# Transposing activations, softmax rows and GLA keys with DMAs on SP's queue instead of TensorE matmuls, in a hybrid decoder layer

## The reference, cut to what matters

```
xn = rmsnorm(x)
q,k,v,gz,og,u,ga,gb = split(xn @ w_in)            # GLA with chunked scan, pooling branch
o  = rmsnorm(GLA(q,k,v,log_sigmoid(gz @ w_gk_up + b)/16)) * silu(og)
h  = x + (sig(ga)*(o @ w_a) + sig(gb)*(pool_mix(u) @ w_b)) @ w_out
h  = h + softmax(rmsnorm(h) @ w_xq @ K_mem^T / 16) @ V_mem @ w_xo
h  = h + relu(rmsnorm(h) @ w_up)**2 @ w_down
y  = rmsnorm(h)
```

## Time and profile before

| what | value |
|---|---|
| median of the runs shown | 1297.88 us |
| lowest of them | 1295.64 us |
| profiled execution | 1297.93 us |
| its span on the slowest core, which the trace shows | 1296.4 us |
| spans of the 8 cores | 1286.1 to 1296.4 us |
| TensorE (PE) busy | 1261.8 us, 97% |
| DVE busy, ACT busy | 655.0 us, 651.5 us |

### The profile page before, as it was taken

One profiled execution on the slowest core, in us unless ns is written; L12 is line 12 of the kernel. 1 busy time (PEld: TensorE's weight loads), 2 busy tenths in 40 slices (PEclk: granted clock), 3 DMA queues, 4 the chain that ended last, 5 costly groups with the idle time before them and its releaser, 6 DMA issues.

```text
span 1296.4 us, 23207 instructions; the slowest of 8 cores (1286.1 to 1296.4 us)
## 1 busy us (share of the span) xinstructions
PE 1261.8 (97%) x8490; PEld 646.2 (50%) x8490; DVE 655.0 (51%) x1088; ACT 651.5 (50%) x1333; POOL 68.4 (5%) x131
## 2 busy tenths in 40 slices
PE   6899999999999999999999999999999999999997
PEld 4444556444455554444544455644455544454453
DVE  3564755241458765444575346723244754444346
ACT  3555966556587743032246278855557753120304
POOL 1110000000000000000000010100100000000000
PEclk7999999999999999999999999999999999999999
DMA  8979369353929569786779596758871333342503
GB/s 173 185 161 181 68 126 184 55 99 71 223 82 227 136 163 163 125 145 137 142 166 203 94 150 120 138 110 138 143 191 35 64 66 66 65 74 58 98 2 138
DMA packets 33675, 160.93 MB, mean 124 GB/s; under 512 B 4598, under 2 KB 5246, under 8 KB 22156
## 3 DMA queue, kind: packets, MB, share of 16 engines
q0 software_dynamic: 18112, 104.29, 48.9%
q1 hardware_dynamic: 15452, 55.15, 12.5%
HBM read 241.63 MB, written 22.80 MB: 204 GB/s over the span
## 4 chain that ended last, share of the span: by engine, by line
PE 93%; DMA 3%; DVE 1%; issue 1%; ACT 1%; DVEq 0%; ACTq 0%; SPq 0%
PE pb L818 83%; PE pb L829 6%; PE pb L849 3%; PE pb L839 1%; DMA land_113<-xp 1%; DMA xst_93<-xp 1%; DMA xst_89<-xp 1%; DMA xst_91<-xp 0%; ACT xn_102 L868 0%; DVE S L889 0%; DVE xh L889 0%; DVE xn_102 L889 0%; DVE xn_101 L889 0%; ACT stat L868 0%; DVE xn_102 L884 0%
## 5 line engine op out<-in xcount | busy, mean ns | idle before, releaser
L889 DVE SCALAR_TENSOR_TENSOR xh<-pb,r_178,xh 128x512 f32<-128x512 f32 x128 | 95.6, 750 | 91.6 <-PE pb L818 91.3
L818 PE MATMUL pb<-actT,wt_45 128*128 128x512 bf16 x448 | 101.4, 379 | 0.0
L818 PE MATMUL pb<-actT,wt_44 128*128 128x512 bf16 x448 | 100.4, 379 | 0.0
L868 ACT ACTIVATE tmp_98<-pb 128x512 f32<-128x512 f32 (+1 forms) x48 | 28.3, 590 | 111.0 <-PE pb L818 108.6
L818 PE MATMUL pb<-actT,wtG 128*128 128x512 bf16 x320 | 72.8, 379 | 0.0
L818 PE MATMUL pb<-actT,wt_43 128*128 128x512 bf16 x320 | 72.5, 379 | 0.0
L818 PEld LDWEIGHTS pb<-actT,wt_45 128*128 128x128 bf16 x448 | 43.1, 98 | 50.5 <-issue 0.4
L818 PEld LDWEIGHTS pb<-actT,wt_44 128*128 128x128 bf16 x448 | 43.1, 98 | 49.7
L878 DVE TENSOR_TENSOR xh<-pb,xh 128x512 f32<-128x512 f32 x64 | 44.2, 691 | 46.8 <-PE pb L818 46.6
L868 ACT ACTIVATE tmp_95<-pb 128x512 f32<-128x512 f32 (+1 forms) x49 | 28.5, 581 | 75.1 <-PE pb L818 60.9
L818 PE MATMUL pb<-wt_45,actT 128*128 128x512 bf16 x256 | 59.3, 379 | 0.6 <-DVE xn_101 L889 0.4
(11 more groups left out here) (559 smaller groups left out, 2378.2 us busy)
## 6 DMA issues: line engine op xcount, KB each, us to landing
wt_44<-wu POOLq DMA_DIRECT2D x19, 1024.0 KB, 10.2
wt_43<-wu POOLq DMA_DIRECT2D x17, 1024.0 KB, 11.6
wt_45<-wu POOLq DMA_DIRECT2D x17, 1024.0 KB, 12.4
wt_46<-wu POOLq DMA_DIRECT2D x16, 1024.0 KB, 11.4
wtG<-wu POOLq DMA_DIRECT2D x13, 1024.0 KB, 11.0
xh<-xp SPq DMA_DIRECT2D x16, 512.0 KB
yp<-xh SPq DMA_DIRECT2D x15, 512.0 KB, 5.0
wt_46<-wscratch SPq DMA_DIRECT2D x2, 1024.0 KB, 24.3
```

What stands on the lines that cost most here:

```text
L818: ins = e.matmul(out, l, r, start=(start and i == 0), stop=(stop and i == m - 1))
L868: return self.g.op("act", lambda e: e.activation(out=out, in_=in_, func=func, scale=scale, **kw), reads=rd, writes=wr, cost=c)
L889: return self.g.op(eng, lambda e: e.scalar_tensor_tensor(out=out, in0=in0, scalar=scalar, in1=in1, op0=op0, op1=op1), reads=rd, writes=[ou ...
```

## The change

All transposes of prompt activations but those of tile 0's input become DMAs with transposition on SP's queue (`dma_start_transpose`), SBUF to SBUF. `actT`, `kd` and `qi` get a layout by row blocks, so that one DMA writes a contiguous 128 x 1024 (keys: 128 x 512); matmuls that read 512 tokens of `actT` now read 4 pieces of 128. The gains that were applied while copying out of PSUM are applied in place in SBUF, by the same engines; copies without a gain vanish. Keys are transposed two chunks ahead. The lags of the stages shrink, `up(0)` runs the first half of the tokens through both weight units before the second half, and the scheduler costs each queue's DMAs apart.

```diff
@@ schedule
-                s = max(t + c + 1.4, dma_free)
-                dma_free = s + o.nb * 1.2
-                o.end = dma_free + 2.0
+                s = max(t + c + 1.4, dfree[e])
+                w = o.nb * 1.2
+                x = max((dfree[q], q) for q in ENGS if q != e)
+                if x[0] > s:
+                    y = min(w, (x[0] - s) / 2)
+                    w += y
+                    dfree[x[1]] += y
+                dfree[e] = s + w
+                o.end = s + w + 2.0
@@ alloc
-        self.actT = g.sb("actT", reg(16384), [128, 8, 1024], BF16)
+        self.actT = g.sb("actT", reg(16384), [128, 8, 8, 128], BF16)
-        self.kd = g.sb("kd", XH, [128, 4, 1024], BF16)
-        self.qi = g.sb("qi", XH + 8192, [128, 4, 1024], BF16)
+        self.kd = g.sb("kd", XH, [128, 8, 4, 128], BF16)
+        self.qi = g.sb("qi", XH + 8192, [128, 8, 4, 128], BF16)
@@ trans_in and transT
+        if self.ti is None:
+            self.transP(xn, self.actT[:, s, :, :], "g_mix")
+        else:
+            self.transT(xn, self.actT[:, s, :, :], "g_mix")
+    def dmaT(self, out, in_):
+        n = self.nfree(in_)
+        return self.g.op("sp", lambda e: e.dma_start_transpose(out=out, in_=in_), reads=[in_], writes=[out], cost=0.07, dma=True,
+                         nb=n / 1024.0)
+    def transT(self, xn, dst, gname=None):
+        self.dmaT(dst, xn[:, :])
+        if gname == "g_gla":
+            for j in range(2):
+                v = dst.rearrange("p (a b) t -> p a b t", b=2)[:, :, j, :]
+                self.cp("act", v, v, scale=self.col("g_gla", j))
+        elif gname is not None:
+            o, w = COLS[gname]
+            self.tt("dve", dst, dst, self.cols[:, o:o + 8].unsqueeze(2).to_broadcast([128, 8, 128]), ALU.mult)
@@ fm
+        if len(src.shape) == 4:
+            return [(u.ap[:, kc, m * 128:(m + 1) * 128], src[:, hf * 4:(hf + 1) * 4, kc, :]) for kc in range(8)]
@@ GLA loop
+        def kdtr(c):
+            kts[c] = self.ring("kdt", self.kdt)
+            self.dmaT(kts[c][:, :, :], self.kd[:, c, :, :].rearrange("p h t -> p (h t)"))
-        scores_kdt(0)
+        kdtr(0)
+        kdtr(1)
+        scores(0)
...
+            if c < 6:
+                kdtr(c + 2)
-            if pend is not None:
-                self.transT(pend[0], None, pend[1], "g_gla")
-            pend = (o2, c)
+            self.transT(o2, self.o2T[:, c, :, :], "g_gla")
@@ T_, PT_, M_ and their loops
-            self.transT(xno[s], A, s, None)
+            self.transT(xno[s], A[:, s, :, :])
-            self.trs([(self.pbf[b][:, j * 128:(j + 1) * 128], Pn[:, j // 2, (j % 2) * 128:(j % 2 + 1) * 128], self.ident[:, :])
-                      for j in range(8)])
-            self.cp("act", pt[:, :, :], self.pbf[b][:, :].rearrange("p (j t) -> p j t", t=128))
+            self.dmaT(pt[:, :, :], pns[s][:, :, :].rearrange("p h m -> p (h m)"))
-            self.transT(xnx[s], A, s, "g_mlp")
-        for t in range(8 + 2):
-            for f, lag in ((T_, 2), (O_, 0)):
+            self.transT(xnx[s], A[:, s, :, :], "g_mlp")
+        for t in range(8):
+            for f, lag in ((O_, 0), (T_, 0)):
-        for t in range(8 + 4):
-            for f, lag in ((M_, 4), (X_, 3), (PT_, 2), (C_, 0)):
+        for t in range(8 + 2):
+            for f, lag in ((C_, 0), (PT_, 0), (X_, 2), (M_, 2)):
@@ up
-                if c + j == 0:
-                    order = [(m, hf) for hf in range(2) for m in range(4)]
+            if c == 0:
+                order = [(j, m, hf) for hf in range(2) for j in range(2) for m in range(4)]
```

More of the change, by code:

```diff
@@ L180, in schedule @@
         done = [False] * len(ops)
-        dma_free = 0.0
+        dfree = {e: 0.0 for e in ENGS}
         def release(o):
@@ L669, in alloc @@
         self.wt.append(g.sb("wtG", G, [128, 8, 512], BF16))
-        self.kdt = [g.sb(f"kdt{i}", G + 1024 * i, [128, 512], BF16) for i in range(2)]
+        self.kdt = [g.sb(f"kdt{i}", G + 1024 * i, [128, 4, 128], BF16) for i in range(2)]
         self.Sb = [g.sb(f"Sb{i}", G + 2048 + 2048 * i, [128, 4, 256], BF16) for i in range(2)]
@@ L1077, in gzp @@
                 b = self.bank()
-                self.mm(self.pb[b][:16, :], [(self.wgz[:, kc, :], A[:, kc, hf * 512:(hf + 1) * 512]) for kc in range(8)])
+                self.mm(self.p3(b, 16), [(self.wgz[:, kc, :], A[:, hf * 4:(hf + 1) * 4, kc, :]) for kc in range(8)])
                 self.cp("act", self.gzT[:, hf * 512:(hf + 1) * 512], self.pb[b][:16, :])
@@ L1154, in uproj, with scores @@
                 self.dma("sp", O["spp"][:, n * 512:(n + 1) * 512], t[113:128, :])
-        ak = {}
-        def scores_kdt(c):
-            cs = slice(c * 128, (c + 1) * 128)
+        ats, kts = {}, {}
+        def kdtr(c):
+            kts[c] = self.ring("kdt", self.kdt)
+            self.dmaT(kts[c][:, :, :], self.kd[:, c, :, :].rearrange("p h t -> p (h t)"))
+        def scores(c):
             att = self.ring("att", self.att)
-            kdt = self.ring("kdt", self.kdt)
             b = self.bank()
-            self.mms([(self.pb[b][:, h * 128:(h + 1) * 128], [(self.kd[:, h, cs], self.qi[:, h, cs])]) for h in range(4)])
+            self.mms([(self.pb[b][:, h * 128:(h + 1) * 128], [(self.kd[:, c, h, :], self.qi[:, c, h, :])]) for h in range(4)])
             self.tt("dve", att[:, :, :], self.pb[b][:, :].rearrange("p (h t) -> p h t", t=128),
                     self.maskT[:, :].unsqueeze(1).to_broadcast([128, 4, 128]), ALU.mult)
[L1165 to L1168, removed]
+            ats[c] = att
         u = self.W("og0")
@@ L1198, in tile @@
             self.tick()
-            att, kdt = ak[c]
+            att, kdt = ats[c], kts[c]
             for hp in range(2):
@@ L1202, in tile @@
                 self.mms([(self.pb[b][:, (h % 2) * 256:(h % 2 + 1) * 256],
-                           [(kdt[:, h * 128:(h + 1) * 128], self.vt[:, c, h * 256:(h + 1) * 256])]) for h in (2 * hp, 2 * hp + 1)])
+                           [(kdt[:, h, :], self.vt[:, c, h * 256:(h + 1) * 256])]) for h in (2 * hp, 2 * hp + 1)])
                 for h in (2 * hp, 2 * hp + 1):
@@ L1209, in tile @@
                         self.cp("dve", self.S[:, h, :], ps)
+            if c < 6:
+                kdtr(c + 2)
             if c < 7:
-                scores_kdt(c + 1)
+                scores(c + 1)
             next(fl)
@@ L1220, in tile @@
                            [(att[:, h, :], self.vt[:, c, h * 256:(h + 1) * 256])]
-                           + ([(self.qi[:, h, cs], Sb[:, h, :])] if have else [])) for h in (2 * hp, 2 * hp + 1)])
+                           + ([(self.qi[:, c, h, :], Sb[:, h, :])] if have else [])) for h in (2 * hp, 2 * hp + 1)])
                 for h in (2 * hp, 2 * hp + 1):
@@ L1332, in C_ @@
                 b = self.bank()
-                self.mm(self.pb[b][:, :], [(A[:, kc, s * 128:(s + 1) * 128], self.WqK[:, kc, hp * 512:(hp + 1) * 512]) for kc in range(8)])
+                self.mm(self.pb[b][:, :], [(A[:, s, kc, :], self.WqK[:, kc, hp * 512:(hp + 1) * 512]) for kc in range(8)])
                 self.redmax(nm[:, 2 * hp:2 * hp + 2], self.pb[b][:, :].rearrange("p (h m) -> p h m", m=256))
@@ L1376, in tile @@
                 self.tick()
-        for t in range(8 + 4):
-            for f, lag in ((M_, 4), (X_, 3), (PT_, 2), (C_, 0)):
-                if 0 <= t - lag < 8 and not (f is M_ and t - lag == 7):
+        for t in range(8 + 2):
+            for f, lag in ((C_, 0), (PT_, 0), (X_, 2), (M_, 2)):
+                if 0 <= t - lag < 8:
                     f(t - lag)
```

61 lines of the change are left out of this document (26 added, 35 removed).

## The result

The changed kernel takes 1450.1 us (median of 4 runs, 1438.7 to 1459.2), the kernel before 1297.2 beside it: ratio 1.118, with a 95% interval of 1.106 to 1.130. It is slower by an eighth, and far outside the range of the forecast.

The account below looks back on a forecast made before the run. TensorE, busy 1261.8 of 1296.4 us, was taken as the bound. From 1297.9 us: minus 36.0 (squares), minus 2 (waits), plus 3 (softmax rows), plus 3 (GLA's output) gives 1266 us; range 1254 to 1318.

Parts of the forecast that it names:

- The squares: TensorE transposes in attention, MLP, GLA and tile 1's input: 640 removed at 56 ns each, 36.0 us of PE.
- The free edits: Gains applied in SBUF instead of from PSUM, and split reads of `actT`, were to cost nothing that shows.
- the 4 us that I took: Time from issue to landing of each transposing DMA, with 2.1 and 17.4 us kept for the range.
- rival A: Transposes land late beside weight loads, 9 us, and give back 30 us: 1290 us; chance 0.20.
- the step: Transposes load the DMA engines with some 20 MB beside 160, so weights keep their room; landing 4 us everywhere.
- Tile 1's input: Between the tiles: 16 groups of `down(3)`, 27.7 us, precede the last block's first reader, so no wait.
- GLA's output: Scalings in ACT's row ahead of copies that free PSUM banks: up to 12 us late in tile 0, 3 us taken.
- Softmax rows: Attention's first values: 2.5 us left for the DMA, so PE waits 1.5 us per tile, 3 us for both.
- rows after w_out: Attention: 7 blocks of 16 matmuls, 24 us, lie between a block's DMA and its scores, so no wait.
- Keys: GLA loops: transposed two chunks ahead, a chunk being 9 us or more, so no wait if SP's queue moves.
- B: SP's queue becomes the bound, each transpose holding it 7 or 8 us: 1321 or 1365 us, slower; chance 0.15.
- C: PE is not the bound in the GLA loops, so 10.8 us of squares removed there don't count: 1279 us; chance 0.10.

Follow-up runs that it names:

- e9: Changed kernel, all its transposes still by DMA, with 66 of 82 weight loads bringing only an eighth of each row (1 KB packets); 1284.9 us, 0.989 of before.
- e1: Changed kernel with all 640 squares back on TensorE; layout, order of the up projection and planner's queue model kept; 1306.5 us.
- e5: Changed kernel with tile 1's input, GLA's output and the keys back on TensorE; 1335.0 us, 1.027 of before.

## Why the prediction was wrong

**Right.** The squares: 640 fewer, 36.0 us of PE, shown by e9's 1226.5 us. The free edits: the gains in place cost 1220 and 716 ns against 1221 and 685 from PSUM, and split reads of `actT` 379 ns (e9), as contiguous ones. A transpose at its quickest: 3.0 us for 256 KB, 2.4 for 128 KB, under the 4 us that I took; 245 GB/s where they stream. The 261 of the Trainium skill ("DMA: Bandwidth & Descriptors", section "Latency and other measured facts") is near that; beside weight loads the landings above are far from it. And the form of rival A: late beside weight loads, idle PE at the first values, in pooling and in GLA.

**Wrong, the step.** "As load on the DMA engines they are some 20 MB beside 160 ..., so weights keep their room", and with it "I take 4 us, between the two cases that had the queue to themselves". The megabytes were right (76.14 - 55.15 = 21.0). But one landing time for all places priced them as if each had the queue to itself, while three of the places lie beside weight loads and there landings of 17 to 64 us were waited for. With 66 of 82 weight loads cut to an eighth the kernel goes from 1450.1 to 1284.9 us, so this step holds some 165 of the 184 us between result and forecast; the rest, 19 us, is what e9 still has over 1266: some 9 for the layout, `up(0)`'s order and the planner (e1), and, not tried apart, landings of up to 11 us.

The trace of before had a row that spoke against 4 us. I read the 17.4 us of `mv` as the price of standing behind 16 small writes. But SP had issued the last of these by 196.44 us, and the next `mv`, issued at 206.65 us beside a weight load into `wtG` and the load from `wscratch`, took longer still:

```profile
mv<-mstage_117 SPq DMA_DIRECT2D x2, 256.0 KB, 26.0
```

So 17 to 26 us for 256 KB on this queue beside megabyte loads stood in the trace of before; how much of it the small writes caused is not shown.

**Wrong with it, place by place.**

- Tile 1's input, "Nothing": 46 us of PE (13.97 and 31.88). I looked for the first reader on PE, 27.7 us later. The first reader is DVE's gain, and in DVE's row the additions that free the banks of `down(2)` stand behind it. The cover of an in-order engine is what stands between the transpose and its first reader on any engine.
- GLA's output, 3 us: PE waited 30.1, 11.1, 8.1 and 7.5 us, together 56.8, for what stood behind ACT's scalings (24.6 us of one wait of ACT for `o2T`, issued at 190.7 us, landed 32.5 us later). The mechanism was named; the size was off by nearly twenty, since I bounded the landing by 12 us late and in one place.
- Softmax rows, 1.5 us per tile: 23.1 us at the first values of tile 1. The DMA stood in SP's queue behind two slow transposes of rows after w_out (28 and 34 us), which themselves hurt nobody: their 24 us of cover, "Nothing", was right for their readers and wrong for the queue behind them. In e5 the wait at this place was 8.9 us.
- Keys, "Nothing, if SP's queue moves": it did not always; 7.9 us.
- The clock had no term. PE's busy time is 1250.9 instead of 1225.8 us: 25 us of matmuls at the 1.2 GHz level behind long waits; with few waits (e9) they are gone.

Against the forecast's span (1296.4 - 32 = 1264.4) the sum is, as a span is PE's busy and idle time: PE idle 206.7 instead of 38.6 us, and 25.1 us more busy, together 193.2 us; 1264.4 + 193.2 = 1457.6. The places above hold 134 of the 168 us of added idle time.

**The rivals.** A had the mechanism, at 9 us a landing and 30 us in all; with 17 to 64 us it is a slower kernel. B forecast slower, but through SP's queue as the steady bound, "PE idle throughout attention". An issue takes 1.2 us when the DMA engines are free and up to 32.6 when they are not; with fewer weight bytes (e9) the same issues end within 3.6, so the queue is held by what loads the engines, not by a steady price of a transpose. In that form B's mechanism did act: the first values of tile 1 waited behind a held SP. Whether C took its 10.8 us no run separates.

## What to carry to other kernels

Price a DMA's landing under the traffic that will run beside it: a queue's share in bytes says little, so look in the trace for the loads that are issued in the same stretch, and if a short transfer has to share with megabyte loads, expect the time of the loads. Follow a new DMA's result to its first reader on any in-order engine, and look at what that engine frees for others behind it. If transposes must go by DMA, keep few loads queued beside them; where TensorE needs 56 ns for a square, there is little to win.

## What was not expected of the hardware

- A transposing DMA is 256-byte packets: 72 x 1024 + 16 x 512 = 81,920 of them, of the 84,736 that SP's queue has more. Alone 980 pass in a microsecond, beside whole weight loads 31 (1254 in 40 us), and the weights themselves are slowed to 2.49 MB in 40 us.
- The stretching goes by the weight bytes beside it first: with most loads cut to an eighth, 16 packets of 8 KB and 128 of 1 KB per load give the same time (1283.8 and 1284.9 us), and with all bytes, one load under way instead of three gives 87 us. With all bytes the size of a packet has a part too: 2 KB and 1 KB instead of 8 KB give 58 and 73 us.
- An issue of such a DMA can hold SP for 32.6 us; where less is queued (e9) none took more than 3.6.
- After an idle stretch of 31.9 us PE was granted 0.51 of its clock for the next 5 us.
